# Modulation sums taken along the partitions instead of along a row

## The reference

```
N_MOD = 6

def modulate(h, shift, scale):
    return h * (1.0 + scale[:, None, :]) + shift[:, None, :]

mod = jax.nn.silu(c) @ w_ada[l] + b_ada[l]            # 1024 x 6144 weights, one row of tokens
sh1, sc1, gt1, sh2, sc2, gt2 = jnp.split(mod, N_MOD, axis=-1)
h = modulate(rms_norm_2(x, norm_mix[l]), sh1, sc1)
...
x = x + gt1[:, None, :] * mix
h = modulate(rms_norm_2(x, norm_ffn[l]), sh2, sc2)
```

## Time and profile before

| What | Value |
|---|---|
| timed runs, median (lowest to highest) | 1640.04 us (1639.43 to 1642.85) |
| profiled execution | 1639.73 us |
| its span, first to last instruction | 1638.4 us |
| TensorE (PE) busy | 1549.2 us, 95% of the span |
| VectorE (DVE) busy | 990.8 us, 60% |
| ScalarE (ACT) busy | 631.1 us, 39% |
| mean granted clock of TensorE | 0.977 of full speed |

### The profile page before, as it was taken

The page is one execution under the profiler, slowest core; times in us unless marked ns, Lnnn a source line. Parts: engine busy times, 40 slices in busy tenths (PEclk is TensorE's granted clock), DMA queues, the critical chain, the costliest instruction groups (busy, mean ns, idle before and its releaser), DMA issues.

```text
span 1638.4 us, 25154 instructions
## 1 busy us (share of the span) xinstructions
PE 1549.2 (95%) x9907; PEld 1284.3 (78%) x9907; DVE 990.8 (60%) x1797; ACT 631.1 (39%) x979; POOL 436.3 (27%) x288
## 2 busy tenths in 40 slices
PE   8999999887999777889899999999999999999998
PEld 5777878673555477448799999999999888888886
DVE  5788787652565663537589863333333677777776
ACT  5465454431221321101343443333333455555453
POOL 0000000000010400000788888888887000000000
PEclk9999999998999797989999999999999999999999
DMA  9776653337465900332566666666765577777776
GB/s 339 249 246 241 238 190 123 123 135 263 151 210 186 400 31 3 116 133 103 155 143 143 144 144 145 143 145 145 144 142 117 177 240 241 240 241 236 241 237 215
DMA packets 165977, 297.23 MB, mean 181 GB/s; under 512 B 49442, under 2 KB 70226, under 8 KB 165860
## 3 DMA queue, kind: packets, MB, share of 16 engines
q1 hardware_dynamic: 119584, 277.08, 50.4%
q0 software_dynamic: 39296, 8.55, 7.4%
q10 hardware_dynamic: 6980, 9.99, 1.8%
HBM read 276.54 MB, written 19.03 MB: 180 GB/s over the span
## 4 chain that ended last, share of the span: by engine, by line
PE 89%; DMA 5%; DVE 3%; issue 2%; ACT 1%; SPq 0%; ACTq 0%; POOL 0%; DVEq 0%
PE bank L494 20%; PE bank L496 20%; PE bank L498 20%; PE bank L489 10%; PE bank L966 7%; PE bank L944 4%; DMA slot<-in_w_in_dram 2%; PE bank L818 1%; PE bank L831 1%; PE bank L546 1%; PE bank L473 1%; DMA slot<-in_expert_down_dram 1%; PE bank L539 0%; PE bank L830 0%; PE bank L743 0%
## 5 line engine op out<-in xcount | busy, mean ns | idle before, releaser
L2242 POOL DMA_INDIRECT c_dram<-gates,places x256 | 404.8, 1581 | 201.5 <-DVE gates L1697 124.2
L494 PE MATMUL bank<-hT_high,dT_high 128*128 128x256 f32 x1024 | 299.6, 293 | 0.0
L1083 DVE TENSOR_TENSOR dT_low<-bank,dT_high 128x512 fp32r<-128x512 f32 x256 | 164.9, 686 | 219.3 <-ACT dT_high L2134 141.2
L496 PE MATMUL bank<-hT_low,dT_high 128*128 128x256 f32 x1024 | 288.7, 282 | 0.0
L498 PE MATMUL bank<-hT_high,dT_low 128*128 128x256 f32 x1024 | 285.2, 279 | 0.0
L496 PE MATMUL bank<-up_low,A_high 128*128 128x512 f32 x512 | 200.7, 392 | 0.0
L494 PE MATMUL bank<-up_high,A_high 128*128 128x512 f32 x512 | 199.9, 390 | 0.4 <-DVE A_low L1083 0.4
L498 PE MATMUL bank<-up_high,A_low 128*128 128x512 f32 x512 | 199.2, 389 | 0.0
L2146 ACT CAST up_high<-slot 128x1024 fp32r<-128x1024 f32 x128 | 134.3, 1049 | 164.8 <-DMA slot<-in_expert_up_dram 164.8
L498 PEld LDWEIGHTS bank<-hT_high,dT_low 128*128 128x128 f32 x1024 | 193.9, 189 | 0.0
L494 PEld LDWEIGHTS bank<-hT_high,dT_high 128*128 128x128 f32 x1024 | 193.4, 189 | 0.0
(11 more groups left out here) (416 smaller groups left out, 2295.7 us busy)
## 6 DMA issues: line engine op xcount, KB each, us to landing
slot<-in_expert_down_dram SPq DMA_DIRECT2D x128, 512.0 KB
slot<-in_expert_up_dram SPq DMA_DIRECT2D x128, 512.0 KB, 3.7
slot<-in_w_in_dram SPq DMA_DIRECT2D x41, 1024.0 KB, 5.2
P<-in_w_ada_dram SPq DMA_DIRECT2D x16, 1024.0 KB, 7.9
c_dram<-zeros SPq DMA_DIRECT2D x1, 16384.0 KB, 50.5
slot<-c_dram SPq DMA_DIRECT2D x128, 128.0 KB, 3.6
slot<-in_w_in_dram SPq DMA_DIRECT2D x7, 2048.0 KB, 7.9
ada_late<-in_w_ada_dram POOLq DMA_DIRECT2D x8, 1024.0 KB, 6.0
```

Source lines behind the costliest of these rows:

```text
L494: pe.matmul(o, lhsT=lhs_high.bitcast(F32R), rhs=rhs_high.bitcast(F32R), start=start, stop=False, skip_group_check=True)
L496: pe.matmul(o, lhsT=lhs_high.bitcast(F32R), rhs=rhs.bitcast(F32R), start=False, stop=False, skip_group_check=True)
L1083: return v.tensor_tensor(dst.bitcast(F32R), src, high, ALU.subtract)
L2242: g.indirect_dma_start(C_dram, bass.IndirectOffsetOnAxis(ap=places[:, x, k:k + 1], axis=0), gates[:, x, k:k + 1], None, compute_op=ALU.add ...
```

## The change

The sum over the partitions is turned round. `pe_ada_columns` makes the 512 columns of `ada_acc` the weights, in four blocks of 128, and moves the column of ones through each: four matmuls of one column, whose results lie along the partitions. `v_ada_columns` adds the bias there and writes straight into `modT`. For this the bias has to lie along the partitions too: the new `a_mod_loads` reads the four bias vectors and the two norm gains with the pattern `(k p) -> p k`, in which neighbouring elements of a partition are 128 elements apart in memory. These six loads are issued in step 1, behind the nine tables, and no longer in step 36. The loads of the bias rows on SyncE, the stores of the rows, the reload, the transpose and its copy are gone.

```diff
+    def pe_ada_columns(r):
+        b = fill(("ada", r), 4 + r % 2)
+        pe.wait_ge(ada_summed, 2 * r + 2)
+        for q in range(4):
+            m = pe.matmul(b[:, q:q + 1], lhsT=ada_acc[r % 2][:, q * P:(q + 1) * P], rhs=col[:, 0:1], start=True, stop=True)
+        m.then_inc(filled(("ada", r)), 1)
...
             if x in row_at:
-                pe_ada_row(row_at[x], 4 + row_at[x] % 2)
+                pe_ada_columns(row_at[x])
...
     def pe_merge():
-        b = side(("modT",))
-        pe.wait_ge(mod_in, 64)
-        pe.transpose(b[:, 0:48], mod_rows[0:48, :], ident[0:48, 0:48]).then_inc(filled(("modT",)), 1)
...
+    def v_ada_columns(r):
+        b = held(v, ("ada", r))
+        if r == 0:
+            v.wait_ge(mod_bias_in, 16 * 6)
+        at = slice(r % 2 * 4, r % 2 * 4 + 4)
+        v.tensor_tensor(modT[:, r // 2, at], b[:, 0:4], mod_bias[:, r // 2, at], ALU.add).then_inc(emptied(("ada", r)), 1)
...
             if x - 1 in row_at:
-                v_ada_row(row_at[x - 1])
+                v_ada_columns(row_at[x - 1])
...
-        b = held(v, ("modT",))
-        v.tensor_copy(modT.rearrange("p a k -> p (a k)"), b[:, 0:48]).then_inc(emptied(("modT",)), 1)
-        clear(v, ("modT",))
+        for r in range(EARLY // 2):
+            clear(v, ("ada", r))
...
-    def a_ada_store(x):
-        if x in row_at:
-            r = row_at[x]
-            clear(a, ("ada", r))
-            a.dma_start(mod_dram[:, mod_at[r]:mod_at[r] + CW], ada_b[r % 2][0:1, :]).then_inc(mod_out[r % 2], 16)
+    def a_mod_loads():
+        for n, g in enumerate((0, 1, 3, 4)):
+            a_load(mod_bias[:, n, :], I["b_ada_2"][0, g * D:(g + 1) * D].rearrange("(k p) -> p k", p=P), mod_bias_in)
+        a_load(modT[:, 4, :], I["norm_mix_2"][0].rearrange("(k p) -> p k", p=P), mod_bias_in)
+        a_load(modT[:, 5, :], I["norm_ffn_2"][0].rearrange("(k p) -> p k", p=P), mod_bias_in)
...
             if x == 1:
                 a_first_loads()
+                a_mod_loads()
...
-            if x == 36:
-                a_mod_loads()
...
-            a_ada_store(x - 2)
...
-    def s_ada_b(r):
-        if r > 1:
-            sp.wait_ge(mod_out[r % 2], 16 * (r // 2))
-        sp.dma_start(ada_b[r % 2][0:1, :], I["b_ada_2"][:, mod_at[r]:mod_at[r] + CW]).then_inc(ada_b_in[r % 2], 16)
```

More of the change, by code:

```diff
@@ L129, in program @@
     tokens_in = [sem("tokens0_in"), sem("tokens1_in")]
-    start_in, first_in, merge_in, mod_in = sem("start_in"), sem("first_in"), sem("merge_in"), sem("mod_in")
+    start_in, first_in, merge_in = sem("start_in"), sem("first_in"), sem("merge_in")
     second_in, third_in, peer_in = sem("second_in"), sem("third_in"), sem("peer_in")
@@ L140, in program @@
     row_at = {ada_x[2 * r + 1] + 1: r for r in range(EARLY // 2)}
-    row_x = list(row_at)
     late_row = {(0, 0): 8, (0, 3): 9, (1, 1): 10}
@@ L144, in program @@
     ada_load = {ada_x[p] + 5: p + 2 for p in range(EARLY - 2)}
-    ada_b_load = {row_x[r] + 6: r + 2 for r in range(EARLY // 2 - 2)}
     SPLIT = 26
     ada_in, ada_late_in = [sem(f"ada{j}_in") for j in range(2)], sem("ada_late_in")
-    ada_b_in, late_b_in, ada_summed = [sem(f"ada_b{j}_in") for j in range(2)], sem("late_b_in"), sem("ada_summed")
+    mod_bias_in, late_b_in, ada_summed = sem("mod_bias_in"), sem("late_b_in"), sem("ada_summed")
     late_out, gt_in = sem("late_out"), sem("gt_in")
@@ L152, in program @@
     h_rounded, h_split, turn_high = sem("h_rounded"), sem("h_split"), sem("turn_high")
-    mod_out = [sem(f"mod_out{j}") for j in range(2)]
     sb_squared, sb_summed, sb_rooted, sb_gated = sem("sb_squared"), sem("sb_summed"), sem("sb_rooted"), sem("sb_gated")
@@ L231, in program @@
     gain1 = carve("gain1", KT)
-    modT = carve("modT", 6, KT)
+    modT, mod_bias = carve("modT", 6, KT), carve("mod_bias", 4, KT)
     lasting_top = cursor[0]
@@ L307, in program @@
     w_hi.append(carve("w_hi3", KT // 2, CW))
-    mod_rows = carve("mod_rows", P)
-    ada_b = [carve(f"ada_b{j}", CW) for j in range(2)]
     for j in range(4):
@@ L353, in program @@
     mla_w = [carve(f"mla_w{j}", 3 * P) for j in range(4)]
-    ada_late, late_b = carve("ada_late", KT // 2, CW), ada_b[1]
+    ada_late, late_b = carve("ada_late", KT // 2, CW), carve("late_b", CW)
     cursor[0] = mla_w_at
@@ L1067, in v_ada_sum @@
         m.then_inc(ada_summed, 1)
+    def v_ada_columns(r):
[4 more added lines that the diff above has]
+        v.tensor_tensor(modT[:, r // 2, at], b[:, 0:4], mod_bias[:, r // 2, at], ALU.add).then_inc(emptied(("ada", r)), 1)
     def v_ada_row(r):
         b = held(v, ("ada", r))
[L1071 to L1077, removed]
+        v.wait_ge(late_b_in, 16 * (r - EARLY // 2 + 1))
+        v.tensor_tensor(late_b[0:1, :], b[0:1, :], late_b[0:1, :], ALU.add).then_inc(emptied(("ada", r)), 1)
     def v_high(dst, src):
@@ L1817, in a_sb_squares @@
             a.activation(sb_sq[:, t], P1[:, t, Q_:K_ + 1, :], ACT.Square).then_inc(sb_squared, 1)
[L1819 to L1825, removed]
     def a_sb_score(i):
@@ L2201, in g_late @@
         held(g, ("out", 1, 0, 1))
-        for j in range(2):
-            g.wait_ge(mod_out[j], 16 * EARLY // 4)
         g_late_bias(8)
@@ L2280, in s_halves @@
                 s_ada(h - 2)
-                s_ada_b(h - 2)
             if h in ada_load:
                 s_ada(ada_load[h])
-            if h in ada_b_load:
-                s_ada_b(ada_b_load[h])
     def s_chunks():
```

## The result

The changed kernel takes 1655.72 us (median of 6 runs, 1653.77 to 1658.04); the kernel before, on the same chip, 1639.74 us (6 runs, 1636.03 to 1642.85). The ratio is 1.0099, with a 95% interval of 1.0082 to 1.0116: about 16 us slower. The forecast was 1651, with a range of 1639 to 1655. The direction was right, and the time is 0.7 us above the range. The profiled execution took 1658.04 us, the slowest of the six, so stages read from it add up to a little more than the medians differ by.

What follows compares the result with a forecast made beforehand. TensorE was taken as the bound. From 1639.73 us, +12.4 for half 5 delayed by ScalarE held issuing six loads, and -0.7 of TensorE's own work, gave 1651.4, forecast as 1651 us; range 1639 to 1655.

Steps and rivals of the forecast that it cites:

- The hold: ScalarE, issuing six single-element loads in step 1, stays held until 44.0 us; half 5 on TensorE begins 12.4 us later.
- the sums' gain: TensorE's eight row sums as four one-column matmuls each, 0.89 us instead of 0.95: -0.5 us.
- What bounds the kernel: TensorE, busy 95% of the span, sets the end; work taken from VectorE, ScalarE or the queues gives nothing by itself.
- VectorE's saving: Eight one-partition additions become 128x4 additions and a copy goes: some 4 us less on VectorE, nothing gained in time.
- VectorE's new wait for the six loads: In step 5 ahead of the split of half 7; a delay up to some 6 us is hidden behind TensorE's matmuls.
- the stores and loads taken off ScalarE and SyncE: Eight bias loads, eight stores and four reloads removed, issues of under 0.5 us: costed at nothing.
- the rival of turns by groups: Eight elements of a partition go per 2 KB packet, 1.3 us a load: +6, 1645.5 us; 0.18 including holds in between.
- the queue that holds all six: ScalarE issues six loads at 0.48 us each, free at 29.3 us, inside the slack: 1639.8 us; chance 0.27.
- From ScalarE to half 5: CAST and split of half 4, its matmuls with 1.8 us clock loss, row 0; half 5 begins at 56.5 us.
- The faster rival: One-column matmuls on TensorE at half the pitch, 0.45 us a sum, eight give 4 us: 1635.4 us; chance 0.05.
- the -0.8 forecast: TensorE's own work: eight sums -0.5 us and the removed transpose of line 643 -0.3 us.
- the likeliest case: ScalarE held until the small packets find an empty queue: 1651 us, own range 1648 to 1655; chance 0.50.

Runs made afterwards that it cites:

- the changed kernel in place: The changed kernel with `mod_bias` carved behind `ret_w`, where it moves no later tile; the six loads stay on ScalarE: 1648.28 us, ratio 1.0050.
- three loads: The kernel before with three single-element loads issued by ScalarE behind the tables, to an unread tile that moves no other: 1647.94 us, ratio 1.0050.

## Why the prediction was wrong

The step that failed is in the sum: it has no term for the tile `mod_bias`, which moves all later tiles by 128 bytes and costs 6.1 us by itself. The hold was sized a little too low and the sums' gain too, and these two errors work against each other.

**What bounds the kernel:** right. TensorE's waits and work account for all of the first block's loss, and no run shows VectorE's saving of 5.7 us busy (985.1 against 990.8) as a gain. VectorE's new wait for the six loads never shows: it takes row 0 at 59.01, released by TensorE. What the stores and loads taken off ScalarE and SyncE gave is not told apart; it is part of what stays open.

**The hold on ScalarE:** right as a mechanism, somewhat undersized. The trace shows six issues of up to 6.09 us, and with the loads given to GpSimd, or made of 32-byte pieces, TensorE's wait before half 4 vanishes. The forecast had ScalarE free at 44.0; it was at 44.66. (The 44.6 that it gave as an upper end is half a us more than its own terms add up to, 41.7 + 2.4.) How it came so near is partly luck. Packets by queue (packets, MB, share of 16 engines), from 36 to 41 us, and then from 41 to 43:

```profile
q1 hardware_dynamic: 882, 1.75, 98.7%
q10 hardware_dynamic: 841, 0.00, 11.7%
```

```profile
q1 hardware_dynamic: 197, 0.37, 52.9%
q10 hardware_dynamic: 1306, 0.01, 38.1%
```

Beside the full stream the small packets go one for one, at 168 a us (forecast 142). Eight small ones for each large one, as the rival of turns by groups had it, is out, also for eight elements a partition; so is the queue that holds all six. Without the stream they came in bursts: 795 in the 0.4 us from 42.0, about 2000 a us and so above the 1600 read from the earlier trace rows, but only 139 from 42.5 to 43.0. The row below is the engines' share in 40 slices, from 42.40 to 44.06 us, while ScalarE was in its fifth issue:

```profile
DMA  9785622010010103168988899799997532101000
```

The engines stand nearly idle twice in it, and ScalarE is held all the same. What it waits for then is not shown. At 41.7 us 1722 of the 6144 packets had gone, where the forecast had 1240, and the 2342 that went between 41.7 and 44.66 took 3.0 us, where it had 2860 to 3880 in 1.8 to 2.4. More gone beside the stream, slower behind it: the two errors nearly cancelled. From 44.7 to 50 us the same queue shows this:

```profile
q10 hardware_dynamic: 2080, 0.01, 21.7%
```

So 2080 of 6144 packets were left when ScalarE came free: two loads outstanding, the fourth just gone, as the forecast had it. But that is no rule for each load: when the third issue ended 1987 packets of the loads issued were outstanding, at the end of the fourth 1558 and of the fifth 1146. The Trainium skill (DMA: Bandwidth & Descriptors, queues, rings and completion order) says that an engine drains typically 9 to 17 descriptors from one ring before it switches. If the turns of both queues hold alike many, that too comes to one for one, so that 882 against 841 packets don't decide it, and the forecast was wrong to take its rival's time from that rule. No run here shows how long a turn is.

**From ScalarE to half 5:** the forecast gave 56.5 us, the trace 58.84. Term by term: the CAST starts 0.8 later. The copy at line 1043 (0.7 us, and 0.6 of the sum) had been put beside the chain as VectorE's own business; it stands in it, since it frees the place for half 4's products. Half 4 lost 2.8 us to the clock where 1.8 was taken, more than the 2.5 of the row at 308.7; in between the engine had executed nothing for 14.8 us. Row 0 took nearly what was said. Sum 0.8 + 0.6 + 1.0 - 0.1 = 2.3. In all, the hold costs 13.4 us in the change and 15.2 and 15.4 us on the kernel before, against the +12.4 forecast; the 13.4 lies within the intervals of the other two.

**The sums:** mis-sized. From the start of the last matmul ahead of a row to the start of the second one behind it, 1.61 us had gone before, and 1.36 go now (57.80 to 59.16): 0.25 us a row, 2.0 for eight, against the 0.5 forecast from line 771. The eight records of a row take what was said; the old row's overlap with its neighbours was worse than that. It is also the reason that 14.7 us at half 5 are 12.9 at the retention. The faster rival was right in its direction. Kernels without hold and move show what the sums are worth with the other removals, against the -0.8 forecast: -2.6 us with the bias as rows, -2.4 with GpSimd's loads and their later start, and -5.7 with the 32-byte pieces.

**The place of later tiles:** the step that failed by being absent. The change was costed instruction by instruction, and a tile that only holds 128 bytes a partition had no term. It costs +6.1 us alone, +5.8 when only the experts' tiles move, and 5.8 and 7.4 when taken back from two versions of the change. Without it the forecast would have held: the changed kernel in place takes 1648.28 us, at the lower end of the likeliest case's own range. That too is partly luck, since there a hold of 13.4 us instead of 12.4 stands against sums and removals of -5.7 instead of -0.8.

**What stays open.** The sums and removals. With the value from the 32-byte pieces, -5.7 us [-7.2, -3.6], the parts add up within the noise: 15.2 (hold) + 6.1 (place) - 5.7 = 15.6 against 16.0 [13.4, 19.0], and in place 15.2 - 5.7 = 9.5 against 7.7 [5.9, 10.7]. With -2.4 in its stead they would be 18.9 and 12.8, the second outside that interval. But most of the 5.7 us is not explained. The first block agrees in all profiles: with the hold the last retention matmul starts at 285.0 (three loads) and at 289.2 to 291.7 (six), without it at 275.3 to 278.8. In the profile of the 32-byte pieces this is 275.3 us, only 1.2 sooner than before, and the stretch from there to about 536 us, which no edit touched, takes 255.6 us instead of 259.9. Over all the profiles this stretch takes 255.5 to 259.9 us, and the next, to about 728 us, 191.1 to 195.4, also between kernels with the same time (195.4 with 256 bytes, 191.7 before). It is not all chance of one execution: the changed kernel in place and the one with 32-byte pieces, whose tiles lie alike, differ by no more than 0.2 us in any stretch behind the retention. Whether these differences come from the place of tiles in the second block, from the removed instructions or in part from chance was not settled.

**Versions that beat both kernels:** among those that compute the same, the new sums with the bias as rows, 1638.12 us, and with GpSimd's loads and `mod_bias` in place, 1638.01 us. The gain is 0.15% and 0.09%, and the second interval touches 1. The loads in 32-byte pieces, at 1634.90, are the fastest, 0.33% below before, and would need `b_ada` and the gains stored in the matching order.

## What to carry to other kernels

Price a load by its pieces, and put the price on the engine that issues it: count what the queue already holds, the stream it shares the DMA engines with, and the first compute instruction behind it, with its slack. The same bytes in longer pieces cost nothing here. Issued by GpSimd at the start they held up no engine, but TensorE's first wait grew by 3.4 to 3.7 us. Follow the late half through everything its consumer needs, the copy that frees its place included. When an edit adds or resizes a tile, every tile behind it moves; compare the mean time of matmuls that the edit doesn't touch, and try the tile at the end, before the logic of the edit is judged.

## What the runs showed of the hardware

- In the changed kernel a load of 1024 single elements behind another held the issuing engine for 4.3 to 6.1 us beside a full stream. GpSimd issued the four bias loads in 3.81 us at the start, 0.95 each, and wasn't held; the load of `cT` beside them took 8.4 us to land instead of 5.1.
- Single elements on one queue and packets of 2 KB on the other went one for one, 841 against 882 in 5 us. Alone, 795 single elements went in 0.4 us.
- Matmuls of 512 columns in an unchanged loop took 389 to 398 ns in the mean, by the place of tiles. Moves of 64 and 128 bytes cost 7.6 and 5.8 us, 192 bytes 0.7, 256 bytes nothing. Why is not shown.
- After 14.8 us without a matmul, 13 of them ran in 5 us at a granted 0.50; the 24 of the half took 2.8 us more than at full clock.
